# Feed-forward seams of a two-layer block: a sum and a copy moved ahead, stores before small loads, weights in halves, the gating's first tile inside the last step

## What is computed

```python
h = rms_norm(x) * (1.0 + scale_a) + shift_a
mix = hybrid_mixer(h, ...)
x = x + gate_a * mix
h = rms_norm(x) * (1.0 + scale_f) + shift_f
x = x + gate_f * (jnp.square(jax.nn.relu(h @ w_mlp_up[l])) @ w_mlp_down[l])
```

## Time and profile before

| | us |
|---|---|
| median of three runs | 3516.66 (3513.88 to 3517.92) |
| profiled execution, its own time | 3516.78 |
| its span, first to last instruction | 3515.5 |
| PE busy | 3379.8 (96%) |
| DVE busy | 2009.8 (57%) |
| ACT busy | 1286.0 (37%) |
| POOL busy | 472.6 (13%) |
| mean granted clock of PE | 0.981 |

### The profile page before, as it was taken

How to read it: one execution, slowest core, us unless ns; L and a number is a source line. 1 busy time by engine, 2 the same in 40 slices (tenths; PEclk the granted TensorE clock), 3 DMA queues, 4 the chain that set the end, 5 groups by cost and what they waited for, 6 DMA issues and landing times. The chain is left out here.

```text
span 3515.5 us, 42813 instructions
## 1 busy us (share of the span) xinstructions
PE 3379.8 (96%) x16731; PEld 2293.9 (65%) x16731; DVE 2009.8 (57%) x3578; ACT 1286.0 (37%) x2245; POOL 472.6 (13%) x575
## 2 busy tenths in 40 slices
PE   7999899899999989998999999999999997999998
PEld 4666567688888866665677887888775683333333
DVE  3666684877757656666848666576664743000002
ACT  2444333455544334443335555443330621111111
POOL 1222110000000002221100000000110002444443
PEclk9999999999999999999999999999999998999999
DMA  6000362355575560003722444754600317887633
GB/s 233 28 28 22 125 248 92 120 177 174 190 257 192 192 223 28 28 22 110 254 91 102 153 154 167 254 193 171 202 15 1 127 61 273 283 307 250 216 96 120
DMA packets 270228, 525.22 MB, mean 149 GB/s; under 512 B 46192, under 2 KB 117560, under 8 KB 263884
## 3 DMA queue, kind: packets, MB, share of 16 engines
q1 hardware_dynamic: 238652, 398.56, 32.4%
q0 software_dynamic: 29920, 123.28, 10.6%
q10 hardware_dynamic: 1456, 0.66, 0.1%
HBM read 615.18 MB, written 114.82 MB: 208 GB/s over the span
## 5 line engine op out<-in xcount | busy, mean ns | idle before, releaser
L226 PE MATMUL psum<-arena_r,arena_r 128*128 128x512 f32 (+1 forms) x5084 | 1213.8, 391 | 24.4 <-ACT arena_r L2179 10.5
L226 PEld LDWEIGHTS psum<-arena_r,arena_r 128*128 128x128 f32 x5084 | 960.0, 190 | 227.3 <-issue 12.5
L226 PE MATMUL psum<-arena 128*128 128x128 f32 (+8 forms) x3834 | 764.8, 376 | 18.5 <-ACT arena L1043 7.6
L226 PEld LDWEIGHTS psum<-arena 128*128 128x128 f32 (+1 forms) x3834 | 468.6, 192 | 270.8 <-issue 193.3
L4373 PE MATMUL psum<-arena 128*64 128x512 f32 x1536 | 341.2, 596 | 6.1 <-DMA arena<-in_expert_w_gate,be_i 5.3
L2312 ACT ACTIVATE arena_r<-arena 128x1024 fp32r<-128x1024 f32 x192 | 192.2, 1051 | 327.4 <-PE psum L226 302.0
L2473 DVE TENSOR_TENSOR arena_r<-arena,arena_r 128x1024 fp32r<-128x1024 f32 x192 | 225.8, 1220 | 135.9 <-ACT arena_r L2312 135.8
L269 POOL TENSOR_SCALAR stat<-stat 128x1 f32<-128x1 f32 (+1 forms) x120 | 36.3, 303 | 1985.4 <-ACT arena L1018 665.4
L4505 DVE TENSOR_TENSOR arena<-arena,psum 128x512 f32<-128x512 f32 x24 | 16.5, 687 | 427.3 <-PE psum L4373 427.3
L234 PEld LDWEIGHTS psum<-const,arena 128*128 128x128 f32 (+1 forms) x1439 | 169.0, 153 | 132.6 <-issue 82.5
L4373 PEld LDWEIGHTS psum<-arena 128*64 128x64 f32 x1536 | 108.8, 137 | 214.7 <-issue 211.0
(11 more groups left out here) (469 smaller groups left out, 3971.8 us busy)
## 6 DMA issues: line engine op xcount, KB each, us to landing
tmp_hidden<-arena SPq DMA_DIRECT2D x224, 256.0 KB, 2.0
arena<-tmp_hidden SPq DMA_DIRECT2D x112, 512.0 KB, 4.8
arena<-in_w_mlp_down SPq DMA_DIRECT2D x96, 512.0 KB, 6.3
arena<-in_w_ada SPq DMA_DIRECT2D x36, 1024.0 KB, 7.7
weight_ring<-in_w_mlp_up SPq DMA_DIRECT2D x32, 1024.0 KB, 5.5
tmp_x_res<-arena SPq DMA_DIRECT2D x32, 512.0 KB, 5.8
arena<-in_w_in SPq DMA_DIRECT2D x6, 2048.0 KB, 14.4
arena<-tmp_x_res SPq DMA_DIRECT2D x24, 512.0 KB, 8.4
```

Source lines behind the costliest of these rows:

```text
L226: i = self.nc.tensor.matmul(out, lhs, rhs, start=start and n == 0, stop=stop and n == len(pairs) - 1, skip_group_check=read_between)
```

## The change

1. `mid` of chunk 0 (DVE) stands right behind the split of product 3, and ACT's copy of product 5's bank right behind ACT's split of product 3; both stood in the chunk's own part.
2. The modulation unit of chunk n and the takes stand at the end of chunk n on DVE, and PE's unit product one chunk later, behind product 3. Unit 15 keeps its place. Units 12 to 15 are taken after the last subtraction of chunk 15.
3. `w_am` and `w_qk` are loaded in two halves over k, in layer 1 with steps 26 to 29.
4. The stores of x tiles 4 to 7 of layer 0 stand ahead of the gate and q_up loads. The mixer waits for the stores of x only at ACT's last copy of the latents and DVE's decay levels of tile 0 (`before_levels`).
5. After layer 1, the turning of the rows and of x tile 0 goes into the last down step, behind bank 1, on bank 3 instead of 5; DVE's part (`dve_gat_first`) stands ahead of the last four additions.

```diff
--- before.py
+++ after.py
@@ -635,6 +635,11 @@
         E.wait_ge(S_.ada_dve.at("take", 0, 3))
     else:
         E.wait_ge(S_.down_pe.at(l - 1, TURNS - 1, 3), S_.down_dve.at("x", l - 1, NT - 1))
+
+
+def before_levels(k, E, l):
+
+    if l > 0:
         for t in range(NT):
             E.wait_ge(x_stored(k, t).at(l - 1))
 
...
 def w_in_of(k, l, first, last):
     return k.d["w_in"][l].rearrange("(k p) n -> p k n", p=P)[:, :, first:last]
 
 
-def sp_mixer_am(k, l):
-    k.nc.sync.dma_start(k.mix.w_am, w_in_of(k, l, C_A, D_IN)).then_inc(*k.S.w_am_in.dma(l))
-
-
-def sp_mixer_qk(k, l):
-    k.nc.sync.dma_start(k.mix.w_qk, w_in_of(k, l, 0, 512)).then_inc(*k.S.w_qk_in.dma(l))
+def sp_mixer_am(k, l, half):
+    k.nc.sync.dma_start(k.mix.w_am[:, at(half, 4), :], w_in_of(k, l, C_A, D_IN)[:, at(half, 4), :]).then_inc(*k.S.w_am_in.dma(l))
+
+
+def sp_mixer_qk(k, l, half):
+    k.nc.sync.dma_start(k.mix.w_qk[:, at(half, 4), :], w_in_of(k, l, 0, 512)[:, at(half, 4), :]).then_inc(*k.S.w_qk_in.dma(l))
 
 
 def sp_mixer_o(k, l):
@@ -1087,6 +1088,8 @@
         s.activation(V.tmp[:, QR:QR + KVR], k.ps[4][:, QR:QR + KVR], ACT.Square, accum_out=st[:, 5:6]).then_inc(*E.up())
         if t > 0:
             E.wait_ge(dve.at("rot", l, t - 1))
+        else:
+            before_levels(k, E, l)
         s.activation(V.pe_in[:, MH, :], k.ps[4][:, QR + KVR:448], ACT.Copy).then_inc(*out.up("m_read", l, t))
         E.wait_ge(dve.at("ebl", l, t))
         s.activation(V.decay, V.decay, ACT.Exp).then_inc(*out.up("decay", l, t))
@@ -1201,6 +1204,8 @@
         for g in range(2):
             v.tensor_tensor_scan(V.b[:, g, :], k.c(K_ONE), V.la[:, g, :], 0.0, ALU.mult, ALU.add).then_inc(*E.up())
         E.wait_ge(E.last)
+        if t == 0:
+            before_levels(k, E, l)
         for lv in range(LEVELS):
             half = 2 ** lv
             bb = V.b.rearrange("p g n -> p (g n)").rearrange("p (n a h) -> p n a h", a=2, h=half)
@@ -1773,6 +1778,8 @@
         act_right_high(k, l, p)
         if p in (3, 7, 4):
             act_up_high(k, l, 0, p)
+        if p == 3:
+            act_up_copy(k, l, 0, 5)
 
 
 def dve_residual(k, l, t):
@@ -1894,9 +1901,13 @@
     dve_up_low(k, l, 0, 6)
     dve_right_low(k, l, 6)
     dve_up_sum(k, l, 0, 7)
-    for p in (3, 7, 4):
-        dve_right_low(k, l, p)
-        dve_up_low(k, l, 0, p)
+    dve_right_low(k, l, 3)
+    dve_up_low(k, l, 0, 3)
+    dve_up_mid(k, l, 0)
+    dve_right_low(k, l, 7)
+    dve_up_low(k, l, 0, 7)
+    dve_right_low(k, l, 4)
+    dve_up_low(k, l, 0, 4)
 
 
 def pool_output(k, l):
@@ -2139,10 +2150,10 @@
         if l + 1 < DEPTH:
             if q == 3 * PASS - 4:
                 sp_mixer_o(k, l + 1)
-            if q == 3 * PASS + 2:
-                sp_mixer_am(k, l + 1)
-            if q == 3 * PASS + 4:
-                sp_mixer_qk(k, l + 1)
+            if q in (3 * PASS + 2, 3 * PASS + 3):
+                sp_mixer_am(k, l + 1, q % 2)
+            if q in (3 * PASS + 4, 3 * PASS + 5):
+                sp_mixer_qk(k, l + 1, q % 2)
             if q == TURNS - 3:
                 E.wait_ge(S_.down_dve.at("x", l, 3))
                 sp_store_x(k, l, 0)
@@ -2154,13 +2165,15 @@
             sp_store_x(k, l, t)
         E.wait_ge(S_.down_pe.at(l, TURNS - 1, 3))
         k.nc.sync.dma_start(k.mix.wkv_up, k.d["w_kv_up"][l + 1]).then_inc(*S_.kv_up_in.dma(l + 1))
+        for t in range(NT // 2, NT):
+            sp_store_x(k, l, t)
         sp_up_weights(k, l + 1)
     else:
         for t in range(4):
             sp_store_x(k, l, t)
         sp_second_ahead(k)
-    for t in range(NT // 2, NT):
-        sp_store_x(k, l, t)
+        for t in range(NT // 2, NT):
+            sp_store_x(k, l, t)
 
 
 def act_up_high(k, l, n, p):
@@ -2263,7 +2276,8 @@
         if n > 0 and more:
             act_up_high(k, l, n + 1, 1)
         act_up_sum(k, l, n, "u11", k.ff.u11[n % 2])
-        act_up_copy(k, l, n, 5)
+        if n > 0:
+            act_up_copy(k, l, n, 5)
         if n > 0 and more:
             act_up_high(k, l, n + 1, 2)
         if more:
@@ -2367,6 +2381,16 @@
     k.nc.vector.tensor_tensor(V.u11[n % 2], V.m1, up_bank(k, n, 1), ALU.add).then_inc(*out.up("c11", l, n))
 
 
+def dve_up_mid(k, l, n):
+
+    S_, E, V = k.S, k.dve, k.ff
+    E.wait_ge(S_.up_pe.at(l, n, 6))
+    if n > 0:
+        E.wait_ge(S_.up_dve.at("c12", l, n - 1))
+    E.wait_ge(S_.up_act.at("copy", l, n, 5))
+    k.nc.vector.tensor_tensor(V.mid, V.m5, up_bank(k, n, 0), ALU.add).then_inc(*S_.up_dve.up("mid", l, n))
+
+
 def dve_up_chunk(k, l, n):
     S_, E, V = k.S, k.dve, k.ff
     v, out, pe, act = k.nc.vector, S_.up_dve, S_.up_pe, S_.up_act
@@ -2380,17 +2404,12 @@
         dve_up_last(k, l, n - 1)
         dve_up_low(k, l, n, 4)
     if l + 1 < DEPTH:
-        if n > 0 and n % 3 == 0:
-            for u in range(n - 3, n):
-                dve_ada_unit_take(k, l + 1, u)
-        dve_ada_unit(k, l + 1, n)
+        if n == FFC - 1:
+            dve_ada_unit(k, l + 1, n)
     if more:
         dve_up_sum(k, l, n + 1, 5)
-    E.wait_ge(pe.at(l, n, 6))
     if n > 0:
-        E.wait_ge(out.at("c12", l, n - 1))
-    E.wait_ge(act.at("copy", l, n, 5))
-    v.tensor_tensor(V.mid, V.m5, b1, ALU.add).then_inc(*out.up("mid", l, n))
+        dve_up_mid(k, l, n)
     if more:
         dve_up_sum(k, l, n + 1, 6)
         dve_up_low(k, l, n + 1, 5)
@@ -2434,6 +2453,11 @@
     v.tensor_tensor(V.s2, V.s1, u11, ALU.subtract).then_inc(*out.up("s2", l, n))
     if more:
         dve_up_low(k, l, n + 1, 7)
+        if l + 1 < DEPTH:
+            if n > 0 and n % 3 == 0:
+                for u in range(n - 3, n):
+                    dve_ada_unit_take(k, l + 1, u)
+            dve_ada_unit(k, l + 1, n)
 
 
 def dve_up_last(k, l, n):
@@ -2524,7 +2548,8 @@
         dve_up_chunk(k, l, n)
     dve_up_last(k, l, FFC - 1)
     if l + 1 < DEPTH:
-        dve_ada_unit_take(k, l + 1, FFC - 1)
+        for u in range(FFC - 4, FFC):
+            dve_ada_unit_take(k, l + 1, u)
     for q in range(1, TURNS):
         if q >= PASS:
             dve_down_turned(k, l, q)
@@ -2535,6 +2560,8 @@
     if l + 1 < DEPTH:
         dve_norm_x(k, l + 1, 0)
         dve_turned_x(k, l + 1, 0)
+    else:
+        dve_gat_first(k)
     for i in range(4):
         dve_down_bank(k, l, 3, i)
 
@@ -2592,8 +2619,12 @@
             ins = k.split_mm(kept_bank(k, i) if first == 0 else fresh_bank(k, i), quads, s == 0 and (stage == 0 or first == 2), s == PASS - 1, stage > 0 and first == 0)
         if s == PASS - 1 or i == 3:
             ins.then_inc(*S_.down_pe.up(l, q, i))
-        if q == TURNS - 1 and i == 1 and l + 1 < DEPTH:
-            pe_turn_x(k, l + 1, 0)
+        if q == TURNS - 1 and i == 1:
+            if l + 1 < DEPTH:
+                pe_turn_x(k, l + 1, 0)
+            else:
+                pe_gat_columns(k)
+                pe_gat_turn(k, 0)
 
 
 def pe_ff(k, l):
@@ -2602,10 +2633,12 @@
             pe_up(k, l, n, 2)
         for p in (5, 6, 3, 7):
             pe_up(k, l, n, p)
+            if p == 3 and 0 < n and l + 1 < DEPTH:
+                pe_ada_unit(k, l + 1, n - 1)
         if 0 < n < FFC - 1:
             pe_up(k, l, n + 1, 1)
         pe_up(k, l, n, 4)
-        if l + 1 < DEPTH:
+        if l + 1 < DEPTH and n == FFC - 1:
             pe_ada_unit(k, l + 1, n)
     for q in range(TURNS):
         pe_down(k, l, q)
@@ -2767,8 +2800,7 @@
 def pe_gat_gate(k, t):
     S_, E, V = k.S, k.pe, k.gat
     E.wait_ge(S_.gat_dve.at("v", t))
-    if t > 0:
-        E.wait_ge(S_.gat_dve.at("sv", t - 1))
+    E.wait_ge(S_.gat_dve.at("sv", t - 1) if t > 0 else ff_done(k))
     for h in range(AH):
         i = k.mm(k.ps[4][:, at(h, HD)], [(V.wsT[:, h, :], V.vv[:, at(h, HD)])])
     i.then_inc(*S_.gat_pe.up("gate", t))
@@ -2781,13 +2813,16 @@
     k.turn([(k.ps[5][:, at(j)], V.ya[:, at(j)]) for j in range(3)]).then_inc(*S_.gat_pe.up("put", t))
 
 
+def pe_gat_columns(k):
+    S_, E, V = k.S, k.pe, k.gat
+    E.wait_ge(S_.cols_in.at())
+    k.turn([(k.ps[3][:, 0:V.n_rows], V.rows[0:V.n_rows])]).then_inc(*S_.gat_pe.up("cols"))
+
+
 def pe_gating(k):
 
     S_, E, V = k.S, k.pe, k.gat
-    E.wait_ge(ff_done(k), S_.cols_in.at())
-    k.turn([(k.ps[5][:, 0:V.n_rows], V.rows[0:V.n_rows])]).then_inc(*S_.gat_pe.up("cols"))
-    pe_gat_turn(k, 0)
-    E.wait_ge(S_.ws_in.at())
+    E.wait_ge(S_.ws_in.at(), S_.gat_dve.at("cols"))
     for n in range(2):
         k.turn([(k.ps[2 + n][:, at(j)], V.ws[:, 3 * n + j, :]) for j in range(3)]).then_inc(*S_.gat_pe.up("ws", n))
     pe_gat_turn(k, 1)
@@ -2955,18 +2990,23 @@
     k.nc.vector.tensor_tensor(V.h_lo[t % 2], k.hT2[:, :, at(t)], V.h_hi[t % 2].bitcast(F32), ALU.subtract).then_inc(*S_.gat_dve.up("low", t))
 
 
-def dve_gating(k):
+def dve_gat_first(k):
+
     nc, S_, E, V = k.nc, k.S, k.dve, k.gat
     dve_gat_norm(k, 0)
     E.wait_ge(S_.gat_pe.at("cols"))
     row = 0
     for _, n, col in V.pieces:
-        i = nc.vector.tensor_copy(k.cols[:, col:col + n], k.ps[5][:, row:row + n])
```

(5 more changed lines are left out.)

24 lines of the change are left out of this document (10 added, 14 removed).

## The result

| | before | changed |
|---|---|---|
| median (14 runs each) | 3517.25 us | 3524.75 us (3520.21 to 3530.78) |
| ratio | | 1.0020 (95% interval 1.0012 to 1.0029) |
| profiled execution, its span | 3516.78, 3515.5 | 3521.13, 3519.8 |

The change costs 7.5 us by the medians, where 1.4 was forecast. The profiled execution of the changed kernel is one of its quicker ones and shows 4.35.

A forecast was written before the change was run, and what follows sets the result against it. It took TensorE (PE), busy 96% of the span, as the bound, so terms count where its next matmul moves. They sum to +1.4 on 3516.78, 3518.2, forecast as 3518.1 us against the median; range 3508.5 to 3524.5.

The forecast's parts named there:

- (b): Last chunk of layer 0: product 4 late and at half clock, down projection waits for the takes; +5.7 us.
- (c): Steps 28 to 31 of layer 0: halved loads end the stall before step 29, step 30 slightly late; -1.7 us.
- (d): Layer 0 to mixer 1: gate product sooner without the wait for stores, -4.7 us, and a clock credit, -0.8.
- (a), layer 0: First chunk of layer 0: product 4 starts 4.0 us sooner but at half clock, +2.0; term -2.0 us.
- (a), layer 1: First chunk of layer 1: product 4 gains 0.15 us, half clock moves to it from product 7; +1.9 us.
- gate loads late: Rival at layer 0 to mixer 1: small gate loads land as late as the stores did; 3523.6 us, chance 0.11.
- (e): Layer 1 to the gating: features start 1.0 us later, then run at half clock, +2.0; term +3.0 us.
- Quick seams: Rival: clock holds at (a) and (e), loads at (b) land in time; -8.7 us, 3508.0, chance 0.20.
- late unit: Rival: modulation unit at the chunk's end makes the next first sum late, 14 chunks; 3532.1 us, chance 0.04.
- No bunching: Rival in layer 0's last chunk: only the first part of (b) falls away; -1.9 us, 3514.8, chance 0.10.

The follow-up runs named there:

- mid_back: The changed kernel with part 1 alone undone (`mid` and ACT's copy of product 5 back in the chunk's own part, both layers): 3519.47 us, ratio 1.0005.
- whole_loads: The changed kernel with both halves of `w_am` issued in step 26 and both of `w_qk` in step 28: 3524.80 us, ratio 1.0019.
- mixing_sooner: The changed kernel with DVE's two mixing-matrix copies and the memset ahead of layer 1's last two bank additions: 3524.47 us, ratio 1.0018.
- unit_load_last: The changed kernel with SP's load of unit n + 1 behind chunk n's four stores instead of ahead of them: 3518.91 us, ratio 0.9998.

## Why the prediction was off by six microseconds

Sign and places were right, and at each of the five the trace shows the wait that the text names. The range held the ratio (3516.66 x 1.0020 = 3523.7; the changed kernel's own median, 3524.75, lies just above the range's 3524.5, on a base that is itself 0.6 higher than the first three runs), and "within 0.2%" had most of the chance. It came out at the very edge of that, 0.20%, since the sum was 6.8 too low on the trace. Staying inside was partly luck: three terms, (b), (c) and (d), missed the same way, 6.6 us together, as much as the range left above the forecast. By its steps, from the profiled execution, with the spread of the other traces where it matters:

- **(a), layer 0** (-2.0, measured -2.5). Product 4 came at 671.46 - 0.93 = 670.5 against 670.8. The wait of 0.6 us for product 6 wasn't there: `mid` ran back to back with the split ahead of it. The half-clock start at product 4 was there; it cost 1.5 us here (24 matmuls in 7.23 instead of 5.7), and up to 2.8 in other traces, which leaves a gain between 0.9 and 2.5.
- **(a), layer 1** (+1.9, measured +2.5). The half clock moved from product 7 to product 4, as written; it cost 2.5 (8.24 instead of 5.7), in the other traces 1.6 to 2.5, so that 2.0 was a fair price. mid_back shows that it is `mid`'s move and nothing else.
- **(b)** (+5.7, measured +9.5). The term that missed by most, in three sizes. The first down load was put at 960.0; it was split at 960.27 in a trace that is 1.4 ahead there, 1.6 later than written, so that product 4 waited 4.69 instead of 3.3. The takes cost what was said: the unit product 2.36 behind product 4. And the second half-clock start, which stood in the text as a bound (+7.5), took place: 0.57 of the clock for 7 us, 2.5 us. I had counted bytes at 406 GB/s on full engines from 951.6 on; the changed kernel's engines moved 345 from 954 to 960 and, by a stretch from 948.90 to 954.30, 255 at a share of 0.76 before that, while SP took 4.89 us to issue the seven stores.
- **(c)** (-1.7, measured -1.2). The stall of 1.56 went; the one behind it was put at step 30 with 0.15 and stands there with 0.66. The rule of the Trainium skill, DMA: Bandwidth & Descriptors, section Bandwidth, that was weighed against the halves did not decide: whole_loads, with both halves in one place, stalls 1.72 at step 29 and 0.20 at step 27, where the undivided loads of the kernel before stalled 1.56 and 0.30. So it is the order that counts, and the halving itself cost nothing that shows. The Trainium skill, Perfetto Trace Analysis, DMA Optimizations, says that "splitting DMAs into smaller sections may allow the overall task to complete sooner", where the engines are idle; the trace agrees in sign, here with busy engines, since what counted was what the halves let pass.
- **(d)** (-5.5, measured -3.2). The gate loads were the next thing late, as said, and PE used them 0.75 later than said (1294.05, in a trace 7.0 behind there, against 1286.3): eight issues took 5.63 us behind the stores instead of 4.10. The credit of 0.8 for the clock came out with the other sign: after 3.63 us of idling PE ran as slow as after 7.55, and for longer (0.55 over 6 us against 0.68), 0.7 us. In the other traces that product took between 1.9 us less than in the kernel before, where the clock held, and 1.1 more, and the whole term lies between -2.5 and -6.2, mostly near -4. The rival "gate loads late" had the mechanism, with 3.6 us of idling where it reckoned with 7.5.
- **(e)** (+3.0, measured +3.1). Right in both halves; what the text did not see is that the weights are right behind: mixing_sooner ran into them.

*Quick seams* failed in all its conditions (the clock at (a) and (e), the loads at (b)), and "late unit" did not happen in the middle chunks (they drifted 0.3 us); at chunk 1 the first sum is late, 1.09 us of waiting instead of 0.84, and 1.84 in mid_back. *No bunching* is refuted by the wait of 4.69 and by unit_load_last. That PE kept its clock in some runs after short gaps is true all the same (below). The Trainium skill, TensorE: Matmul & The Clock Gate, Part 1, says of the point of the transition that it varies from run to run, and these traces agree: 2.02 us of idling ahead of product 5 left the clock at 1.00 in layer 0 of the changed kernel and brought it to 0.58 over four us in layer 1. At product 4 of the first chunks, behind 5.2 to 5.5 us, it fell in every trace with the early `mid`.

## What to carry to other kernels

Before moving work off a seam, ask which idle stretch it leaves in front of the matmul that everything waits for: short waits spread over several matmuls mostly cost their length, one wait of 3.6 us or more cost 1.2 to 3.1 us more in these traces. A step that waits on an engine's queue takes with it whatever stands behind it: here a load's wait held four stores back, and three tiny copies held a whole phase. Test a repair together with what is next behind it: mixing_sooner alone gained 0.6 us until the weights, too, came sooner. And read a stretch of 1 to 3 us in more than one trace before you put a price on it.

## What was not expected of the hardware

The lower clock is no function of the idle time alone. The same product in two runs, the gate product behind 3.32 us of idling (unit_load_last) and behind 3.23 (mid_back), four us from its start:

```profile
1292.53:1296.53 4.00, 4.00 (x13) 2.09 (x14) 0.61 (x2) 0.00 (x0) 0.00 (x0) 1.00 0.82 315
```

```profile
1292.71:1296.71 4.00, 4.00 (x9) 2.35 (x10) 0.61 (x2) 0.00 (x0) 0.00 (x0) 0.59 0.82 315
```

The longer gap kept 2.4 GHz, the shorter fell to 1.2. In the 14 traces every gap of 3.6 us and more in these seams ended at the lower clock, gaps of 1.84 to 2.04 did either, the four of 2.05 to 2.22 kept full clock, and of those from 2.36 to 3.32 only the longest did. And the 0.60 of the earlier trace rows after 2.03 us cost next to nothing: the three products there take 9.9 us with full clock (652.65, 3.01 for twelve) and 10.1 without it, since DVE's splits pace them.
